# A new order for the instructions between the two projections of a token mixer, written by hand on four engines

## The chip, the core and the metric

One core of one Trainium2 chip runs the whole program. Its engines are TensorE (PE in the profile), VectorE (DVE), ScalarE (ACT), GpSimd (POOL) and SyncE (SP), and each has its own list of instructions that runs strictly in order. Engines wait for each other on semaphores. The metric is the device time of one execution in microseconds, taken as a median of several runs.

## What is computed

One inference step of a decoder with two layers, for 256 prompt tokens and 32 sample tokens (8 samples of 4), with shared weights. Each layer is a gated FFN, a token mixer and a second gated FFN. The mixer projects the tokens once, runs three groups of heads on the result and projects once more:

```python
gq, gk, gv, gg, glr, mu, mv, sq, sk, sv = split_cols(a @ w_in)
o_gla, s_gla = gla_mixer(gq, gk, gv, gg, glr, gla_w2, gla_b, gla_nw, gla_s0)
o_gm, v_gm = gmlp_mixer(mu, mv, gm_ln_w, gm_ln_b, gm_ws, gm_bs)
...
o_sb = sb_attend(hs(sq), kk, vv, pos0, sb_b).reshape(B, L, SB_W)
o = jnp.concatenate([o_gla, o_gm, o_sb], axis=-1) @ w_out
```

`gla_mixer` is gated linear attention in chunks of 64 tokens with a matrix state. `gmlp_mixer` is a causal spatial gate over chunks of 128. `sb_attend` is stick-breaking attention: with z the logits and a causal mask, the weights are `exp(log_sigmoid(z) + suffix)`, where `suffix` is the reverse running sum of `-softplus(z)`. Sample tokens attend to 1024 earlier keys and values of their own, which are gathered from a paged cache by a page table (8 heads, 64 wide, pages of 128 keys).

## The kernel before

All products run on TensorE; weights arrive as fp32, and ACT and DVE split each block into `w_hi` and `w_lo` (L1315, L1697), so that three products (L604 to L606) stand for one. Tokens lie along the free dimension, 288 of them (T). PSUM has eight banks, written `PS[:, bank, ...]`.

The change touches the stretch of each layer that lies between the last step of the mixer's input projection and the first product of its output projection (`first_out`, L666). Each of PE, ACT and DVE has an order written out by hand there, with helpers for each piece. No planner or queue chooses anything at run time. The helpers that the text names:

- Samples, in two groups of four samples, g = 0 and 1. DVE `sample_cap(g)`, ACT `sample_log1p_exp(g)` and DVE `sample_sums(g)` (the reverse scans, L1981) make the softplus and its running sums; PE `part_offsets(g)` and DVE `sample_offsets(g)` add the sums of later pages. ACT `sample_weights(g)` takes the exponential (L1475), DVE `turn_weights(g)` transposes in 32x32 blocks (L2001), PE `regroup(g)` moves blocks between partitions (L933), and ACT `weights_by_page(g)` copies the result to `a_keys` (L1482).
- PE `value_chunk(n)`, n = 0 to 15, eight of each group (L956): 4 pages of cached values times `a_keys`, summed in bank 4. Chunk n lies in slot n % 4 of the tile `direct`. SP's `page_chunk` (L486) issues four transfers of 256 KB for chunk n + 4 when chunk n has been used. `new_values(g)` (L967) adds the new tokens' values and ends the group; ACT `sample_rows(g)`, PE `turn_rows(g)` and ACT `sample_heads(g)` bring it into `Y`.
- Prompt, in four pairs of heads, p = 0 to 3. PE, DVE and ACT `prompt_scores(p)` (L1050, L2072, L1545), DVE `prompt_cap(p)`, ACT `prompt_log1p_exp(p)` (L1552, L1554), DVE `prompt_softplus(p)` (L2087), PE `prompt_sums(p)` (L1059, L1060), DVE `prompt_less(p)` (L2093), ACT `prompt_weights(p)` (L1559), PE `prompt_values(q)` (L1070, L1072).
- Linear attention: the gated q and k (L2100 to L2102), `gla_rows` (transposes of values and keys), the masked `att` (L1135, L2123), the state S (L1156, L2136 to L2141), the outputs in bank 6 and 7 (L1188 to L1207, 112 small products), their squares' sums (L1224, L1225), ACT's reciprocal root (L1366, L1368), and the samples' new state (L1242, L2188).
- Spatial gate: transposes of `dm` (L1099, L1105) and of the weights `wsr` (L1110), their mask (L2114), products (L1161, L1169, L1176), bias and gate (L2151, L2155, L2158).
- `rows_of(i, f0, bank, done)` (L1079) transposes 128 (or 32) tokens of keys or values; ACT `key_rows` and `value_rows` copy them out. GpSimd sends them to DRAM once the third copy of a kind is made, and the prompt's state once it is ready.

A wait names what must be done. Two kinds matter here: data, and PSUM banks that hold something still to be read (banks 0 to 3 serve the scores, `regroup`, `att`, the spatial gate and the prompt sums in turn).

## Time and profile before

| | us |
|---|---|
| median of 3 runs | 1393.45 |
| lowest and highest | 1392.14, 1394.14 |
| the profiled execution, its own time | 1392.76 |
| its span, first to last instruction | 1391.0 |
| stretch of the change, layer 0 | 384.36 to 447.69 |
| stretch of the change, layer 1 | 1058.27 to 1122.14 |
| mean granted clock of TensorE | 0.981 of full |

Times inside the trace count from the start of the span. "Idle before" is the time for which an engine had nothing to run before a group, and the name behind the arrow is what released it. A row "x64" of PE is 64 matmul records; an fp32 product is recorded as two. Ends of matmuls overlap the next start, so the distance from start to start is what a group costs.

### The profile page before, as it was taken

Reading aid. Unit: us, or ns where it says so; the run is one execution under the profiler, and the core shown is the slowest. Engines: PE = TensorE matmul, PEld = TensorE weight load, DVE = VectorE, ACT = ScalarE, POOL = GpSimd, SP = SyncE. Lnnn points to the kernel's source line nnn. Section 1 sums busy time; section 2 is a strip of 40 time slices with the busy share of each in tenths; the row PEclk is TensorE's granted clock in tenths of the full one; section 3 lists DMA queues with packets and bytes.
Section 4 is the critical chain, followed back from the end, with each engine's and each line's share of the span. In section 5 each row is a group of like instructions: output and inputs, shape, how many; then the busy total and the mean of one; then the engine's idle time right before and its main releaser. Section 6 shows DMA issues by size and latency. Waiting matters only on the chain.

```text
span 1391.0 us, 34449 instructions
## 1 busy us (share of the span) xinstructions
PE 1330.5 (96%) x13990; PEld 1269.4 (91%) x13990; DVE 810.3 (58%) x1188; ACT 587.9 (42%) x965; POOL 50.6 (4%) x131
## 2 busy tenths in 40 slices
PE   5999999999989899999999999999998998999997
PEld 4899999899966899999989999998997687999997
DVE  2554554668894655555465555447779557555544
ACT  2532243543565543333453333345336555333442
POOL 4000000000020000000000000001001000000000
PEclk9999999999999999999999999999999998999998
DMA  9978779789989895568876567987997993655552
GB/s 330 273 228 260 218 244 319 216 252 338 289 270 325 256 306 152 159 179 270 264 225 173 153 171 223 294 250 219 334 309 231 328 303 89 168 165 160 145 162 82
DMA packets 423816, 324.49 MB, mean 233 GB/s; under 512 B 15559, under 2 KB 351719, under 8 KB 423696
## 3 DMA queue, kind: packets, MB, share of 16 engines
q1 hardware_dynamic: 421124, 317.03, 75.1%
q0 software_dynamic: 2272, 5.61, 1.3%
q8 instruction: 90, 1.47, 0.4%
q14 instruction: 30, 0.25, 0.1%
q10 hardware_dynamic: 300, 0.13, 0.0%
HBM read 317.93 MB, written 4.78 MB: 232 GB/s over the span
## 4 chain that ended last, share of the span: by engine, by line
PE 85%; DVE 6%; ACT 3%; DMA 2%; SPq 2%; DVEq 2%; issue 1%; ACTq 0%
PE PS L604 23%; PE PS L605 23%; PE PS L606 23%; PE PS L632 3%; PE PS L910 2%; PE PS L666 2%; PE PS L667 1%; PE PS L668 1%; PE PS L956 1%; ACT Y L1373 1%; ACT xsq L1387 1%; DMA direct<-in_cache_sb_v 1%; SPq L486 1%; DMA raw<-in_ffn_w_in 1%; DMA xtok<-in_x_sample 1%
## 5 line engine op out<-in xcount | busy, mean ns | idle before, releaser
L1697 DVE TENSOR_TENSOR w_lo<-raw,w_hi 128x1024 fp32r<-128x1024 f32 (+1 forms) x368 | 392.9, 1106 | 443.6 <-ACT w_hi L1315 443.4
L1315 ACT ACTIVATE w_hi<-raw 128x1024 fp32r<-128x1024 f32 (+1 forms) x368 | 337.7, 960 | 659.3 <-PE PS L606 577.9
L604 PE MATMUL PS<-a_hi,w_hi 128*128 128x288 f32 x1760 | 524.0, 298 | 1.3 <-issue 1.3
L605 PE MATMUL PS<-a_lo,w_hi 128*128 128x288 f32 x1760 | 519.2, 295 | 0.0
L606 PE MATMUL PS<-a_hi,w_lo 128*128 128x288 f32 x1760 | 517.5, 294 | 0.0
L604 PEld LDWEIGHTS PS<-a_hi,w_hi 128*128 128x128 f32 x1760 | 329.8, 187 | 3.6 <-issue 3.3
L605 PEld LDWEIGHTS PS<-a_lo,w_hi 128*128 128x128 f32 x1760 | 330.4, 188 | 1.6 <-issue 1.4
L606 PEld LDWEIGHTS PS<-a_hi,w_lo 128*128 128x128 f32 x1760 | 331.4, 188 | 0.0
L605 PE MATMUL PS<-h_lo,w_hi 128*128 128x288 f32 x704 | 208.4, 296 | 0.0
L604 PE MATMUL PS<-h_hi,w_hi 128*128 128x288 f32 x704 | 208.1, 296 | 0.0
L606 PE MATMUL PS<-h_hi,w_lo 128*128 128x288 f32 x704 | 208.0, 296 | 0.0
L604 PEld LDWEIGHTS PS<-h_hi,w_hi 128*128 128x128 f32 x704 | 133.7, 190 | 0.4 <-issue 0.4
L606 PEld LDWEIGHTS PS<-h_hi,w_lo 128*128 128x128 f32 x704 | 132.0, 188 | 0.0
L605 PEld LDWEIGHTS PS<-h_lo,w_hi 128*128 128x128 f32 x704 | 131.9, 187 | 0.0
L1963 DVE STREAM_TRANSPOSE direct<-direct 128x2048 f32<-128x2048 f32 x32 | 72.2, 2289 | 0.0
L632 PE MATMUL PS<-direct,cT 128*32 128x128 f32 x1920 | 65.1, 289 | 7.0 <-issue 3.6
L632 PEld LDWEIGHTS PS<-direct,cT 128*32 128x32 f32 x1920 | 55.1, 117 | 12.3 <-issue 6.6
L666 PE MATMUL PS<-a_hi,w_hi 128*128 128x288 f32 x160 | 49.5, 309 | 5.5 <-DVE a_lo L1934 5.2
L667 PE MATMUL PS<-a_lo,w_hi 128*128 128x288 f32 x160 | 47.9, 299 | 0.0
L668 PE MATMUL PS<-a_hi,w_lo 128*128 128x288 f32 x160 | 47.8, 299 | 0.0
L1836 DVE TENSOR_TENSOR h_lo<-hf,h_hi 128x288 f32 (+1 forms) x88 | 40.3, 458 | 11.5 <-issue 9.5
L1831 DVE TENSOR_TENSOR hf<-sg,PS 128x288 f32<-128x288 f32 x88 | 39.4, 447 | 0.0
(323 smaller groups left out, 1131.0 us busy)
## 6 DMA issues: line engine op xcount, KB each, us to landing
raw<-in_ffn_w_in SPq DMA_DIRECT2D x176, 512.0 KB, 5.0
direct<-in_cond_w SPq DMA_DIRECT2D x240, 256.0 KB, 5.0
direct<-in_cache_sb_k SPq DMA_DIRECT2D x128, 256.0 KB, 4.3
direct<-in_cache_sb_v SPq DMA_DIRECT2D x128, 256.0 KB, 4.3
raw<-in_ffn_w_out SPq DMA_DIRECT2D x64, 384.0 KB, 3.8
raw<-in_mix_w_in SPq DMA_DIRECT2D x48, 512.0 KB, 7.0
raw<-in_ffn_w_out SPq DMA_DIRECT2D x64, 320.0 KB, 4.5
side<-in_cond_w SPq DMA_DIRECT2D x48, 256.0 KB, 5.3
```

The costliest lines, as they stand in the source:

```text
L604: pe.matmul(out, whi, hi, start=begins and i == 0, stop=False)
L605: pe.matmul(out, whi, lo, start=False, stop=False)
L606: last = pe.matmul(out, wlo, hi, start=False, stop=ends and i == n - 1)
L632: last = pe.matmul(PS[32 * g:32 * g + 32, 6 + pair, c * P:c * P + P], cT[:, 4 * half + kb, :], rows[:, kb * 512 + g * P:kb * 512 + g * P + P],
L666: pe.matmul(out, whi, a_hi[:, k, :], start=k == 0, stop=False)
L667: pe.matmul(out, whi, a_lo[:, k, :], start=False, stop=False)
L668: last = pe.matmul(out, wlo, a_hi[:, k, :], start=False, stop=k == KB - 1)
L1315: act.activation(w_hi[:, s, at_:at_ + n], raw[:, s, at_:at_ + n], ACT.Copy)\
L1697: tt(w_lo[:, s, at_:at_ + n], raw[:, s, at_:at_ + n], w_hi[:, s, at_:at_ + n], ALU.subtract).then_inc(lo_done.sem, 1)
L1831: tt(hf[:, s:s + 1, :], sg[:, s:s + 1, :], PS[:, 2 * s + 1:2 * s + 2, 0:T], ALU.mult)\
L1836: tt(h_lo[:, at_, :], hf[:, s:s + 1, :], h_hi[:, at_, :], ALU.subtract)\
L1963: dve.transpose(direct[:, n % 4, :], direct[:, n % 4, :]).then_inc(k_turned.sem, 1)
```

## The change

Only orders and waits change, and one PSUM location. No product, copy or transfer is added or dropped, and no shape changes; one drain of DVE between the spatial gate's bias and its gate goes, as other work now lies between them.

- PE: `regroup(0)` goes ahead of the second `rows_of` and its wait is for the second pair's scores, not for all four. `prompt_scores(2)` and `(3)` go behind it. `value_chunk(0)` goes ahead of `gla_rows` and of `att`; chunks 1 to 13 are spread anew. `part_offsets(1)` goes ahead of the samples' spatial gate. Chunks 5 to 7, `new_values(0)` and `regroup(1)` go ahead of the linear attention's outputs. `prompt_sums(0)`, `(1)` go behind them.
- The spatial gate's small sum for samples moves from bank 5 to bank 7, columns 256 on.
- ACT: `sample_weights(0)` ahead of the prompt scores, `weights_by_page(0)` ahead of the second `key_rows`, `sample_rows(0)` and `weights_by_page(1)` ahead of `value_rows(0)`; `values_by_sample` split into two calls with other work between them; `prompt_log1p_exp(2)` last before the root.
- DVE: `turn_weights(0)` ahead of the gated q and k, the spatial gate's copies and mask ahead of `prompt_scores(2)`, `sample_cap(1)` behind them, the masks of `att` ahead of `sample_sums(1)` (the scans), `sample_offsets(1)` and `turn_weights(1)` ahead of the state S, `prompt_softplus(0)` behind it, `prompt_less(0)` behind the outputs' squares.

```diff
@@ TensorE
-                prompt_scores(2)
-                prompt_scores(3)
                 pe.wait_ge(off_added.sem, off_added.at(l, 1))
...
                 rows_of(0, SK, 4, k_t)
+                pe.wait_ge(zp_off.sem, zp_off.at(l, 2))
+                regroup(0)
                 pe.wait_ge(kv_k.sem, kv_k.at(l, 1))
                 rows_of(1, SK, 4, k_t)
+                pe.wait_ge(a_copied.sem, a_copied.at(l, 1))
+                prompt_scores(2)
+                pe.wait_ge(kv_k.sem, kv_k.at(l, 2))
+                rows_of(2, SK, 4, k_t)
+                prompt_scores(3)
+                value_chunk(0)
+                pe.wait_ge(ws_got.sem, ws_got.at(l, 1))
+                turn_new(0)
                 pe.wait_ge(gla_in.sem, gla_in.at(l, 1))
                 pe.wait_ge(vn_got.sem, vn_got.at(l, 1))
                 gla_rows(0, 6)
-                pe.wait_ge(vn_got.sem, vn_got.at(l, 2))
-                gla_rows(1, 7)
                 pe.wait_ge(zp_off.sem, zp_off.at(l, PR))
-                regroup(0)
...
-                rows_of(2, SK, 4, k_t)
-                pe.wait_ge(gvk_a.sem, gvk_a.at(l, 1))
-                gla_rows(2, 6)
-                value_chunk(0)
-                value_chunk(1)
...
                 last.then_inc(att_sum.sem, 1)
+                pe.wait_ge(vn_got.sem, vn_got.at(l, 2))
+                gla_rows(1, 7)
+                value_chunk(1)
+                pe.wait_ge(gvk_a.sem, gvk_a.at(l, 1))
+                gla_rows(2, 6)
+                value_chunk(2)
                 pe.wait_ge(new_spread.sem, new_spread.at(l, 1))
                 rows_of(2, SV, 5, v_t)
-                value_chunk(2)
+                value_chunk(3)
...
-                value_chunk(3)
+                value_chunk(4)
...
                 last.then_inc(gs_sum.sem, 1)
+                value_chunk(5)
+                part_offsets(1, 5)
                 pe.wait_ge(wss_ready.sem, wss_ready.at(l, 1))
...
                 last.then_inc(gs_sum.sem, 1)
-                part_offsets(1, 5)
-                prompt_sums(0, 0)
-                value_chunk(4)
+                value_chunk(6)
+                value_chunk(7)
+                new_values(0)
+                pe.wait_ge(gm_y.sem, gm_y.at(l, 2))
+                regroup(1)
+                pe.wait_ge(off_added.sem, off_added.at(l, 2))
+                rows_of(0, SV, 5, v_t)
...
                 last.then_inc(o_sum.sem, 1)
-                value_chunk(5)
-                pe.wait_ge(gm_y.sem, gm_y.at(l, 2))
-                prompt_sums(1, 2)
-                pe.wait_ge(off_added.sem, off_added.at(l, 2))
-                rows_of(0, SV, 5, v_t)
-                value_chunk(6)
-                value_chunk(7)
-                pe.wait_ge(c_sub.sem, c_sub.at(l, 2))
-                regroup(1)
-                new_values(0)
+                value_chunk(8)
+                prompt_sums(0, 0)
                 pe.wait_ge(kv_v.sem, kv_v.at(l, 2))
                 rows_of(1, SV, 5, v_t)
+                value_chunk(9)
+                prompt_sums(1, 2)
+                value_chunk(10)
...
                 turn_new(1)
+                value_chunk(11)
                 pe.wait_ge(new_spread.sem, new_spread.at(l, 2))
                 turn_rows(0)
-                value_chunk(8)
+                pe.wait_ge(c_sub.sem, c_sub.at(l, 1))
                 prompt_sums(2, 0)
-                value_chunk(9)
-                value_chunk(10)
-                value_chunk(11)
+                value_chunk(12)
+                pe.wait_ge(c_sub.sem, c_sub.at(l, 2))
                 prompt_sums(3, 2)
...
-                value_chunk(12)
                 value_chunk(13)
@@ ScalarE
+                sample_weights(0)
                 prompt_scores(0)
                 prompt_scores(1)
-                sample_weights(0)
                 key_rows(0, 4)
+                weights_by_page(0)
                 key_rows(1, 4)
+                key_rows(2, 4)
...
                 gla_rows(0, 6)
-                weights_by_page(0)
-                key_rows(2, 4)
+                gla_rows(2, 6)
                 prompt_log1p_exp(0)
-                gla_rows(2, 6)
                 value_rows(2, 1)
                 prompt_log1p_exp(1)
-                values_by_sample()
+                values_by_sample(0)
                 sample_weights(1)
+                sample_rows(0)
+                weights_by_page(1)
                 value_rows(0, 2)
+                values_by_sample(1)
+                value_rows(1, 3)
                 prompt_log1p_exp(2)
-                weights_by_page(1)
-                sample_rows(0)
-                value_rows(1, 3)
@@ VectorE
                 prompt_scores(0)
                 prompt_scores(1)
-                sample_cap(1)
+                turn_weights(0)
                 dve.wait_ge(gate_e.sem, gate_e.at(l, 1))
...
-                turn_weights(0)
-                prompt_scores(2)
-                prompt_scores(3)
...
                    causal[:, :].unsqueeze(1).to_broadcast([P, GH, P]), ALU.mult).then_inc(ws_got.sem, 1)
+                prompt_scores(2)
+                prompt_scores(3)
+                sample_cap(1)
+                prompt_cap(0)
+                prompt_cap(1)
...
                 spread_new(0)
-                sample_sums(1)
-                prompt_softplus(0)
                 dve.wait_ge(att_sum.sem, att_sum.at(l, 1))
...
                 last.then_inc(att_ready.sem, 1)
+                sample_sums(1)
+                dve.wait_ge(wss_sum.sem, wss_sum.at(l, 1))
...
+                sample_offsets(1, 5)
...
+                turn_weights(1)
                 dve.wait_ge(s_sum.sem, s_sum.at(l, 1))
...
                 last.then_inc(s_ready.sem, 1)
...
+                prompt_softplus(0)
                 tt(Y[:, 2:4, :], Y[:, 2:4, :], Fm[:, MU:MU + 2, :], ALU.mult).then_inc(gm_done.sem, 1)
-                sample_offsets(1, 5)
                 prompt_softplus(1)
-                prompt_less(0)
-                prompt_cap(2)
-                turn_weights(1)
...
                 tt(gt[2][:, :, :], gt[0][:, :, :], gt[0][:, :, :], ALU.mult).then_inc(o_sq.sem, 1)
+                prompt_less(0)
+                prompt_cap(2)
                 prompt_less(1)
                 prompt_cap(3)
```

Ahead of `sample_offsets(1)` DVE now has the mask of the samples' spatial weights, and behind it the two bias additions, which it had behind the state S before.

## Rows read from the trace of the kernel before

**Rows 1.** Page, engines: busy time, share of the span, instructions.
```profile
PE 1330.5 (96%) x13990; PEld 1269.4 (91%) x13990; DVE 810.3 (58%) x1188; ACT 587.9 (42%) x965; POOL 50.6 (4%) x131
```
**Rows 2.** Windows over both stretches: length, busy per engine, PEclk, DMA share, GB/s.
```profile
384.30:447.60 63.30, 56.06 (x960) 41.10 (x958) 44.33 (x78) 37.30 (x81) 9.27 (x15) 0.92 0.89 296
1058.20:1122.10 63.90, 56.54 (x960) 41.57 (x958) 44.01 (x78) 37.37 (x82) 9.30 (x15) 0.92 0.89 296
```
**Rows 3.** Timeline of PE, layer 0: start, us, group, idle before and releaser.
```profile
394.68 0.66 PE L1086 MATMUL PS<-ident,Fm 128*128 128x128 f32 x2 [2.56 <-DVE vn L2108]
...
399.67 2.17 PE L956 MATMUL PS<-direct,a_keys 128*32 128x128 f32 x64
...
411.10 1.08 PE L956 MATMUL PS<-direct,a_keys 128*32 128x128 f32 x32
412.11 1.09 PE L1188 MATMUL PS<-att,gvk 128*64 128x128 f32 x16
...
416.29 1.09 PE L956 MATMUL PS<-direct,a_keys 128*32 128x128 f32 x32
...
433.69 0.91 PE L1059 MATMUL PS<-sn,suffix 128*128 128x384 f32 x2
...
435.62 1.93 PE L1242 MATMUL PS<-vm,gvk 32*64 32x512 f32 x8
...
440.31 1.08 PE L956 MATMUL PS<-direct,a_keys 128*32 128x128 f32 x32 [1.62 <-DMA direct<-in_cache_sb_v]
...
447.69 0.40 PE L666 MATMUL PS<-a_hi,w_hi 128*128 128x288 f32 x1
```
**Rows 4.** Timeline of PE, layer 1.
```profile
1113.60 1.94 PE L956 MATMUL PS<-direct,a_keys 128*32 128x128 f32 x32 [1.53 <-DMA direct<-in_cache_sb_v]
...
1118.62 0.44 PE L1072 MATMUL PS<-zp,sv 128*64 128x128 f32 x4
...
1122.14 0.37 PE L666 MATMUL PS<-a_hi,w_hi 128*128 128x288 f32 x1 [0.21 <-DVE a_lo L2203]
```
**Rows 5.** Timeline of ACT, layer 0.
```profile
388.49 1.06 ACT L1475 ACTIVATE z<-z 128x1024 f32<-128x1024 f32 x1
...
397.89 1.21 ACT L1482 ACTIVATE a_keys<-PS 128x256 f32<-128x256 f32 x4 [0.71 <-PE PS L933]
...
426.56 0.69 ACT L1366 ACTIVATE gt<-PS,eps 128x512 f32<-128x512 f32 x1 [0.28 <-PE PS L1225]
...
431.56 0.84 ACT L1554 ACTIVATE sn<-sn 128x768 f32<-128x768 f32 x1
```
**Rows 6.** Timeline of DVE, layer 0.
```profile
391.16 1.23 DVE L2001 STREAM_TRANSPOSE a_turn<-z 128x1024 f32<-128x1024 f32 x1
...
432.44 0.96 DVE L2087 SCALAR_TENSOR_TENSOR sn<-zp,sn 128x768 f32<-128x768 f32 x1 [0.84 <-ACT sn L1554]
...
438.20 0.95 DVE L2093 SCALAR_TENSOR_TENSOR zp<-zp,PS 128x768 f32<-128x768 f32 x1
```
**Rows 7.** SP's line L486 over chunk 4's issues, then over chunk 10's, with landing times.
```profile
L486 SPq DMA_DIRECT2D direct<-in_cache_sb_v x4: 333/356/358, 401.2 to 402.8; - x4
...
DMA to landing us min/median/max: 3.8/4.2/4.8
...
L486 SPq DMA_DIRECT2D direct<-in_cache_sb_v x4: 332/333/333, 422.6 to 424.1; - x4
...
DMA to landing us min/median/max: 2.7/3.4/4.6
```
**Rows 8.** Windows before and in two stretches of lower clock, columns as in the second group.
```profile
413.80:417.20 3.40, 3.40 (x114) 3.17 (x108) 1.85 (x4) 0.00 (x0) 0.00 (x0) 1.00 1.04 379
417.20:420.60 3.40, 3.40 (x15) 2.08 (x8) 0.27 (x1) 0.00 (x0) 0.00 (x0) 0.50 0.64 152
...
1110.10:1113.50 3.40, 1.63 (x36) 0.81 (x32) 1.98 (x3) 1.22 (x2) 0.00 (x0) 1.00 1.03 381
1113.50:1116.90 3.40, 3.30 (x42) 2.45 (x44) 0.00 (x0) 1.52 (x2) 0.00 (x0) 0.51 1.05 357
```

More of the change, by code:

```diff
@@ L1160, in _ @@
                 pe.sem_inc(gvk_seen.sem, 1)
-                pe.matmul(PS[0:NS, 5, 0:GH * TS], rep[:, :, :].rearrange("s b t -> s (b t)"),
+                pe.matmul(PS[0:NS, 7, 256:256 + GH * TS], rep[:, :, :].rearrange("s b t -> s (b t)"),
                           wst[0:TS, :, 0:TS], start=True, stop=True).then_inc(wss_sum.sem, 1)
-                value_chunk(3)
+                value_chunk(4)
                 pe.wait_ge(att_ready.sem, att_ready.at(l, 2))
@@ L1574, in key_rows, with values_by_sample @@
                     act.activation(kst[0:n, i, :], PS[0:n, bank, :], ACT.Copy).then_inc(kv_k.sem, 1)
-                def values_by_sample():
-                    for j in range(GP):
-                        for b in range(B):
-                            last = act.activation(vm[j][:, b, :], gvk[0:NS, 2, j * P:j * P + P], ACT.Copy,
-                                                  scale=same_s[:, b:b + 1])
-                        last.then_inc(vm_ready.sem, 1)
+                def values_by_sample(j):
+                    for b in range(B):
+                        last = act.activation(vm[j][:, b, :], gvk[0:NS, 2, j * P:j * P + P], ACT.Copy,
+                                              scale=same_s[:, b:b + 1])
+                    last.then_inc(vm_ready.sem, 1)
                 def sample_rows(g):
@@ L2110, in _ @@
                 cp(vn[0:NS, 2, :], PS[0:NS, 7, 0:GW]).then_inc(vn_got.sem, 1)
-                prompt_cap(0)
-                prompt_cap(1)
                 dve.wait_ge(ws_t.sem, ws_t.at(l, 1))
@@ L2131, in _ @@
                 last.then_inc(att_ready.sem, 1)
+                sample_sums(1)
+                dve.wait_ge(wss_sum.sem, wss_sum.at(l, 1))
+                tt(wss[:, :, :].rearrange("s h (b t) -> s h b t", t=TS),
+                   PS[0:NS, 7, 256:256 + GH * TS].rearrange("s (h t) -> s h t", h=GH).unsqueeze(2)
+                   .to_broadcast([NS, GH, B, TS]),
+                   same_s[:, :].unsqueeze(1).unsqueeze(3).to_broadcast([NS, GH, B, TS]), ALU.mult)\
+                    .then_inc(wss_ready.sem, 1)
+                sample_offsets(1, 5)
+                dve.wait_ge(bs_in.sem, bs_in.at(l, 1) * 64)
+                dve.wait_ge(gs_sum.sem, gs_sum.at(l, 1))
+                tt(Y[:, 2:4, 0:NP].rearrange("p j (i t) -> p j i t", i=PT_),
+                   PS[:, 2, :].rearrange("p (i j t) -> p j i t", i=PT_, j=GP),
+                   bs[:, :, :].unsqueeze(2).to_broadcast([P, GP, PT_, P]), ALU.add).then_inc(gm_y.sem, 1)
+                dve.wait_ge(gs_sum.sem, gs_sum.at(l, 2))
+                tt(sample(Y, 2, 4), PS[:, 3, 0:GP * NS].rearrange("p (j b t) -> p j b t", j=GP, t=TS),
+                   bs[:, :, 0:TS].unsqueeze(2).to_broadcast([P, GP, B, TS]), ALU.add).then_inc(gm_y.sem, 1)
+                turn_weights(1)
                 dve.wait_ge(s_sum.sem, s_sum.at(l, 1))
@@ L2142, in _ @@
                 last.then_inc(s_ready.sem, 1)
-                dve.wait_ge(wss_sum.sem, wss_sum.at(l, 1))
-                tt(wss[:, :, :].rearrange("s h (b t) -> s h b t", t=TS),
-                   PS[0:NS, 5, 0:GH * TS].rearrange("s (h t) -> s h t", h=GH).unsqueeze(2)
-                   .to_broadcast([NS, GH, B, TS]),
-                   same_s[:, :].unsqueeze(1).unsqueeze(3).to_broadcast([NS, GH, B, TS]), ALU.mult)\
-                    .then_inc(wss_ready.sem, 1)
-                dve.wait_ge(bs_in.sem, bs_in.at(l, 1) * 64)
-                dve.wait_ge(gs_sum.sem, gs_sum.at(l, 1))
-                tt(Y[:, 2:4, 0:NP].rearrange("p j (i t) -> p j i t", i=PT_),
-                   PS[:, 2, :].rearrange("p (i j t) -> p j i t", i=PT_, j=GP),
-                   bs[:, :, :].unsqueeze(2).to_broadcast([P, GP, PT_, P]), ALU.add).then_inc(gm_y.sem, 1)
-                dve.wait_ge(gs_sum.sem, gs_sum.at(l, 2))
-                tt(sample(Y, 2, 4), PS[:, 3, 0:GP * NS].rearrange("p (j b t) -> p j b t", j=GP, t=TS),
-                   bs[:, :, 0:TS].unsqueeze(2).to_broadcast([P, GP, B, TS]), ALU.add).then_inc(gm_y.sem, 1)
-                dve.drain()
+                prompt_softplus(0)
                 tt(Y[:, 2:4, :], Y[:, 2:4, :], Fm[:, MU:MU + 2, :], ALU.mult).then_inc(gm_done.sem, 1)
-                sample_offsets(1, 5)
                 prompt_softplus(1)
-                prompt_less(0)
-                prompt_cap(2)
-                turn_weights(1)
                 dve.wait_ge(o_sum.sem, o_sum.at(l, 1))
```

3 lines of the change are left out of this document (removed).

## The prediction

> **What bounds the kernel now.** I read the page's engine rows first: TensorE is busy for 96% of the span [rows 1], so time is won only where TensorE waits or runs slowly. Then the windows over the two stretches that the change touches. They last 63.3 and 63.9 us, 9% of the span together. TensorE is busy for 56.1 and 56.5 us of them, and its granted clock there is 0.92 [rows 2]: the mean of 2.4 GHz and of some 10 us at 1.2 GHz. So in each stretch 7.3 us are idle, and up to 5 us of the busy time are lost to the low clock. The timeline of PE says where. In layer 0 it stands 2.56 us for a copy of DVE before `gla_rows(0)`, and 1.62 us near the end for a value chunk's transfer [rows 3]; layer 1 has 1.53 us of the latter [rows 4]. The other waits are under 0.9 us each.
>
> The transfers are a second chain. SP may ask for chunk n + 4 only when chunk n is used. The first chunk starts at 399.67 and takes 1.0 us, half of the pair's row [rows 3]; SP's next request goes out at 401.2 [rows 7]. Behind the stretch, the output projection and the FFN are products back to back, so a microsecond won at the first product of the output projection, 447.69 in layer 0 and 1122.14 in layer 1 [rows 3, 4], is won in full. I subtract 673.91, the distance between the stretches' starts, from layer 1's times: its 1122.14 is then 448.23.
>
> **The change, followed through.** Nothing is computed less. I lay the new orders out with start-to-start distances of this trace: an instruction starts when its engine is free and its last wait is over, some 0.05 us after the releaser's end. All times are layer 0's, at the full clock.
>
> *Up to the first chunk.* PE's part offsets, first two scores and 14 transposes are packed from 384.4 to 388.3. ACT now does `sample_weights(0)` right behind the gates' exponentials, at 387.15 (388.49 before, 1.06 us and a small one [rows 5]), to 388.3. DVE turns them at 388.4 instead of 391.16 (1.23 us [rows 6]), to 389.6. PE regroups for 0.5 us, ACT copies for 1.2 us [rows 5], to 391.5. Then PE has two scores of 0.75 us, a transpose group of 0.45 between them and a wait of 0.15: `value_chunk(0)` at 393.7, 6.0 us before today's 399.67. SP's next request falls at 395.1 instead of 401.2.
>
> *Up to the outputs of the linear attention.* PE waits 0.65 us for ACT's `gla_rows(0)`, which lies behind two activations of 1.05 us for samples. Chunks 1 to 4 start at 397.4, 399.5, 400.9 and 402.7. Then the transfers are late. An unloaded chunk needs 1.5 us from first to last issue and up to 4.6 from there to landing, 6.1 in all [rows 7]. Chunk 4 shares the engines with GpSimd's copy of the keys, which goes out about 0.9 us ahead of it now as then: 1.6 + 4.8 = 6.4 us [rows 7]. Loaded, the engines move 379 GB/s [rows 8], so chunks of 1.05 MB land 2.7 to 2.8 us apart. Chunk 4 lands at 401.6, chunk 5 at 405.0 (3.4 us later, the keys' copy taking its share), 6 at 407.8, 7 at 410.5. PE waits some 0.3, 0.8 and 1.7 us for 5, 6 and 7, which it uses early now. Chunk 7 (1.0), `new_values(0)`, `regroup(1)` and a transpose (2.2 us) follow, so the outputs start at 413.7. DVE is no bound there: the state is ready at 412.1.
>
> *The Trainium skill on this point.* "DMA: Bandwidth & Descriptors" gives about 2.0 us of fixed cost for one transfer (section "Anatomy of one DMA") and about 358 GB/s from DRAM for one core (section "Specifications"). An estimate by it is 2.0 + 1.05 MB / 358 GB/s = 4.9 us for an unloaded chunk. The trace has 6.1 us [rows 7], and under load a higher rate [rows 8]. By the page's figure chunk 7 would land some 0.8 us earlier, and the sum below would be 1.6 us better over two layers. I go by the rows.
>
> *From the outputs to the end.* The 112 small products take 416.29 - 412.11 = 4.2 us [rows 3]: to 417.9. Then chunk 8, prompt sum 0, a transpose group, chunk 9, sum 1, chunk 10 (3 x 0.97 + 2 x 1.9 + 0.45 = 7.2 us; a sum is 435.62 - 433.69 [rows 3]) and the squares' sums, 1.0 us, end at 426.1. Today they end at 426.3, just before ACT's root [rows 5], so up to here the transfer waits have eaten the 6 us. From here a chain through ACT and DVE rules: root, two weights, sample heads and `prompt_log1p_exp(3)`, from 426.56 to 432.40 today [rows 5], then softplus, 0.96 us [rows 6]. It reaches the last prompt sum at 426.1 + 0.2 + 5.9 + 1.0 = 433.2, with PE idle for 2.1 us ahead of it (today 433.69). That sum and the states' product (1.9 + 1.93 us [rows 3]) end at 437.0. `prompt_less(3)` ends 439.15 - 437.55 = 1.6 us behind the latter [rows 3, 6], at 438.6; ACT's weights last to 439.5; the second `prompt_values` starts at 439.7 (0.1 us for the semaphores) and takes 1.35, to 441.0. From its end to `first_out`, a path of rounding through ACT and DVE, lie 1122.14 - 1119.0 = 3.15 us [rows 4]; PE's last chunks (2.9 us) fit in. Result: 444.2. The gain is 3.5 us in layer 0 and 4.0 us in layer 1, 7.5 together. Nearly all of it is the transfer waits at today's end, with the slow stretch behind layer 1's: chunks 12 to 15 are now asked for over 5 us before they are needed.
>
> *The clock.* This sum has no slow stretch. Today the clock fell to half in both layers behind the small products of the outputs, in layer 0 from 417.2 to 420.6 [rows 8], though TensorE was busy without a break before. At half speed 3.4 us delay full work by 1.7 us. The new order leaves the 112 products in one block, so I take one such stretch per layer, -3.4 us. What remains is 7.5 - 3.4 = 4.1 us. Bounds: none (7.5), and one more in each layer (below).
>
> *Moved at no cost.* GpSimd's copies of keys, values and state follow their tiles; the keys' copy is counted above, the others lie in the transfers' spare time. If they did not, each takes 0.6 MB / 379 GB/s = 1.5 us. The output weights' split on ACT waits for those copies, which end earlier. `values_by_sample` in two parts costs nothing: ACT stands idle for over 4 us before `value_rows(1)`. `wss` in bank 7 meets nothing that is still read.
>
> **The rivals.**
> A: as laid out, one slow stretch per layer; 4.1 us faster.
> B: fewer slow stretches, or chunks 6 and 7 in time. For it: `regroup` and two scores now break up the run of transposes ahead of today's first slow stretch; and without the transfer waits the outputs would start with the state at 412.1 instead of 413.7, 1.6 us per layer. Against it: rows 7 and 8. 5.7 to 7.5 us faster.
> C: the transfer wait brings a slow stretch. The waits for chunks 6 and 7 leave PE two thirds idle for 3.4 us, and in layer 1 the clock was 0.51 right behind such a stretch with its wait of 1.53 us [rows 4, 8]. One fall more in each layer costs 0.8 to 1.6 us (the table's shift, by where it begins), 2.4 together: 1.7 us faster, within what can be told from no change.
> D, the other side: the clock. If it falls more often than today, in the early block of transposes and scores too (1.4 to 2.4 us per layer, as the first chunk then comes that much later or the end of the block runs at half speed) and behind the transfer waits, that is 2.4 + 3 to 5 us more than A: 1.3 to 3.3 us slower. It decides from three falls per layer on. Against it: that block is 6 us shorter than today's.
>
> **How the numbers follow.** The profiled execution took 1392.76 us, 1.76 more than its span; the median is 0.69 above it. A gives 1392.76 - 4.1 = 1388.7 for such an execution, and 1393.45 - 4.1 = 1389.4 against the median. Chances: A 0.38, B 0.20, C 0.27, D 0.15. A measurement of this kernel can tell about 0.2%, 2.8 us, from no change. A (but for 0.05, a little less gained) and B are faster by that: 0.53. C, that 0.05 and the milder third of D are within it, 0.36 with rounding; slower is 0.11. The range reaches from B's 1393.45 - 7.5 = 1386.0 to D's milder end, 1393.45 + 1.3 = 1394.8.
>
> **What the profile would show.** Chunk 0 near 393.7 and SP's next request near 395; waits for transfers before chunks 6 and 7, and none before 12 to 15; the outputs (L1188) near 413.7; a clock of 0.5 behind them; the squares' sums ending at 426 to 428; PE idle for about 2 us before the last prompt sum; `first_out` at 444 to 446. The forecast is wrong if chunk 0 is late, if chunk 7 lands far from 410.5, or if the clock falls in more or fewer places.

## The result, and the profile after

The changed kernel takes 1405.32 us (median of 4 runs, 1402.98 to 1406.27) against 1393.12 us (4 runs, 1392.14 to 1394.14): a ratio of 1.0094, 95% interval 1.0082 to 1.0107. It is 0.9% slower; the forecast was 1389.4, at most 1394.8. Here and below a ratio and its interval are over the fast executions of both kernels, so it can differ by up to 0.15% from the quotient of the two medians beside it. The profiled execution took 1404.54 us, 11.8 more than that of before. The page's row of the engines, which answers to [rows 1], has 10 us more of busy TensorE for the same 13990 matmuls:

```profile
PE 1340.7 (96%) x13990; PEld 1274.7 (91%) x13990; DVE 810.0 (58%) x1188; ACT 587.6 (42%) x965; POOL 50.8 (4%) x131
```

Windows of the changed kernel: both stretches of the change (these answer to [rows 2]), then three places in them in order of time, each the piece ahead of a slow stretch and the slow stretch itself, and last the end of layer 1's. The columns are those of [rows 2].

```profile
386.47:454.70 68.23, 60.50 (x960) 42.62 (x958) 43.60 (x76) 37.06 (x81) 9.41 (x15) 0.87 0.84 277
1065.28:1133.80 68.52, 59.41 (x960) 42.06 (x958) 43.53 (x76) 36.99 (x81) 9.43 (x15) 0.90 0.84 279
...
409.50:412.90 3.40, 1.34 (x40) 0.96 (x38) 2.90 (x4) 1.16 (x2) 0.00 (x0) 0.99 0.98 346
412.90:416.30 3.40, 2.98 (x58) 1.87 (x62) 3.18 (x10) 0.00 (x0) 0.74 (x2) 0.50 1.05 402
419.70:423.10 3.40, 3.40 (x111) 3.11 (x106) 1.48 (x3) 1.75 (x6) 0.00 (x0) 1.00 0.99 369
423.10:426.50 3.40, 3.40 (x12) 2.16 (x9) 0.20 (x1) 0.00 (x0) 0.00 (x0) 0.50 0.65 196
...
436.80:440.20 3.40, 1.25 (x23) 0.74 (x12) 1.40 (x2) 2.14 (x3) 0.00 (x0) 0.99 1.04 396
440.20:450.40 10.20, 10.20 (x63) 5.40 (x62) 2.24 (x3) 2.73 (x3) 0.00 (x0) 0.50 0.38 130
1116.00:1119.40 3.40, 1.25 (x20) 0.75 (x12) 1.36 (x2) 2.10 (x3) 0.00 (x0) 1.00 1.06 393
1119.40:1129.60 10.20, 10.20 (x65) 5.40 (x65) 2.24 (x3) 2.74 (x3) 0.00 (x0) 0.50 0.38 129
```

Counted up to `first_out`, 0.3 to 0.4 us behind the end of these windows, the stretches have grown from 63.3 and 63.9 us to 68.6 and 68.9. TensorE's granted clock in them is 0.87 and 0.90, where both had 0.92. Summed over the granted-clock records, TensorE ran at 1.2 GHz for 17.1 us of the one and 13.7 us of the other, against 10.2 us in each before. The slow stretches are five over both layers in either kernel; they have become longer. The longest is new: 10.2 us at the end of each layer's stretch, during which TensorE had work without a break, behind a piece of 3.4 us in which it had work for only 1.25.

The timeline of PE in the changed kernel, layer 0 (answers to [rows 3]; L1197 is what was L1188, L1246 what was L1242):

```profile
396.03 1.08 PE L956 MATMUL PS<-direct,a_keys 128*32 128x128 f32 x32
...
407.55 1.08 PE L956 MATMUL PS<-direct,a_keys 128*32 128x128 f32 x32 [0.88 <-DMA direct<-in_cache_sb_v]
...
410.17 1.08 PE L956 MATMUL PS<-direct,a_keys 128*32 128x128 f32 x32 [0.41 <-DMA direct<-in_cache_sb_v]
413.32 1.94 PE L956 MATMUL PS<-direct,a_keys 128*32 128x128 f32 x32 [2.07 <-DMA direct<-in_cache_sb_v]
...
417.94 1.09 PE L1197 MATMUL PS<-att,gvk 128*64 128x128 f32 x16
...
431.10 1.13 PE L1228 MATMUL PS<-gt,head_ones 128*128 128x512 f32 x2
...
439.41 0.88 PE L1059 MATMUL PS<-sn,suffix 128*128 128x384 f32 x2 [2.15 <-DVE sn L2090]
...
442.36 3.68 PE L1246 MATMUL PS<-vm,gvk 32*64 32x512 f32 x8
...
455.04 0.37 PE L666 MATMUL PS<-a_hi,w_hi 128*128 128x288 f32 x1 [0.21 <-DVE a_lo L2205]
```

and the same in layer 1, which answers to [rows 4]:

```profile
1088.57 1.08 PE L956 MATMUL PS<-direct,a_keys 128*32 128x128 f32 x32 [1.69 <-DMA direct<-in_cache_sb_v]
...
1093.82 1.08 PE L956 MATMUL PS<-direct,a_keys 128*32 128x128 f32 x32 [1.53 <-DMA direct<-in_cache_sb_v]
...
1118.57 0.88 PE L1059 MATMUL PS<-sn,suffix 128*128 128x384 f32 x2 [2.15 <-DVE sn L2090]
...
1121.43 3.68 PE L1246 MATMUL PS<-vm,gvk 32*64 32x512 f32 x8
...
1134.20 0.37 PE L666 MATMUL PS<-a_hi,w_hi 128*128 128x288 f32 x1 [0.21 <-DVE a_lo L2205]
```

All orders came out as written down: chunk 0 lies 9.6 us after the stretch's start (15.3 before), the transfer waits at the end are gone, and those before chunks 5 to 7 are there. What is new is the price of the wait before the last prompt sum. It is 2.15 us long, as forecast. But 0.8 us behind its end the clock falls, and the states' product behind it takes 3.68 us instead of 1.93.

Counted from each stretch's own start (386.47 and 1065.28), set against the forecast's (its times less 384.36):

| us from the stretch's start | forecast | layer 0 | layer 1 |
|---|---|---|---|
| chunk 0 | 9.3 | 9.6 | 9.6 |
| linear attention's outputs begin | 29.3 | 31.5 | 31.8 |
| squares' sums begin | 40.7 (full clock) | 44.6 | 45.0 |
| last prompt sum begins | 48.8 | 52.9 | 53.3 |
| `first_out` | 59.8 | 68.6 | 68.9 |

Of the 11.8 us, 10.3 lie in the two stretches (5.2 and 5.1). The other 1.5 us are a later start of layer 0's stretch, by 2.1 us, less 0.3 us between the stretches and 0.3 behind them. The change doesn't touch that early part, and in other executions of kernels with the same code there the stretch began between 384.7 and 387.4.

### The profile page after: what moved, and what is told of

Same layout as the page of the kernel before. It is cut to its first block, busy times and chain, and to the rows that moved or that the text cites. A ratio compares the mean times of both kernels' runs of the same rounds, so it can differ in the third digit from the quotient of the medians.

```text
span 1402.8 us, 34451 instructions
## 1 busy us (share of the span) xinstructions
PE 1340.7 (96%) x13990; PEld 1274.7 (91%) x13990; DVE 810.0 (58%) x1188; ACT 587.6 (42%) x965; POOL 50.8 (4%) x131
## 4 chain that ended last, share of the span: by engine, by line
PE 84%; DVE 4%; ACT 4%; DMA 3%; SPq 3%; issue 1%; DVEq 1%; ACTq 0%
PE PS L604 23%; PE PS L605 22%; PE PS L606 22%; PE PS L632 3%; PE PS L666 2%; SPq L486 2%; PE PS L910 1%; PE PS L667 1%; PE PS L668 1%; PE PS L956 1%; ACT Y L1376 1%; ACT xsq L1390 1%; PE PS L1059 1%; DVE w_lo L1700 1%; DMA direct<-in_cache_sb_v 1%
## 5 line engine op out<-in xcount | busy, mean ns | idle before, releaser
L632 PE MATMUL PS<-direct,cT 128*32 128x128 f32 x1920 | 68.4, 298 | 5.9 <-issue 3.7
L956 PE MATMUL PS<-direct,a_keys 128*32 128x128 f32 x1024 | 36.7, 289 | 7.4 <-DMA direct<-in_cache_sb_v 7.4
```

Source lines behind the costliest of these rows:

```text
L632: last = pe.matmul(PS[32 * g:32 * g + 32, 6 + pair, c * P:c * P + P], cT[:, 4 * half + kb, :], rows[:, kb * 512 + g * P:kb * 512 + g * P + P],
L956: last = pe.matmul(PS[32 * p:32 * p + 32, 4, smp * P:smp * P + P], a_keys[:, 4 * half + t, 32 * p:32 * p + 32], direct[:, n % 4, 512 * t + ...
```

## The experiments

Three theories were set against each other. The *clock*: new waits and light work bring TensorE to 1.2 GHz more often and for longer. The *chain*: what ACT and DVE still have to do sets the end, and the clock only shows it. The *transfers*: value chunks that arrive late delay all that follows. Every ratio is against the kernel before on the same chip.

"Filler" below is a 128x128 by 128x256 fp32 product of constants into a PSUM bank that is free at that time; nothing reads it. It is pure extra work for TensorE.

**Chunks in the wait.** The changed kernel, with two value chunks ahead of the last prompt sum.

```diff
                 value_chunk(12)
+                value_chunk(13)
+                value_chunk(14)
                 pe.wait_ge(c_sub.sem, c_sub.at(l, 2))
                 prompt_sums(3, 2)
...
-                value_chunk(13)
...
-                value_chunk(14)
```

> The changed kernel with value chunks 13 and 14 moved ahead of the last prompt sum, into the 2.15 us for which TensorE waits there. Theory 1 (the wait lets the clock fall, and the states' product behind it is too light to bring it back, so 10.2 us run at half speed in each layer): the clock stays at 1.0 up to the output projection and about 4 to 5 us per layer come back, 1395 to 1398 us against 1405.3. Theory 2 (the chain through ACT and DVE sets the end whatever the clock): within 1 us of 1405.3. Theory 3 (late transfers, chunks 4 to 7): no change either, 1404 to 1406.

Measured: 1400.72 us against 1390.85, ratio 1.0066 (1.0047 to 1.0085), less gain than the 1395 to 1398 that the clock theory expected; the time alone hardly sets it apart from the changed kernel (1.0079 when that ran again, below). The profile does. The wait for DVE shrinks to at most 0.2 us (in layer 0 chunk 14 now waits 0.88 us for its transfer there), and there is no slow stretch behind it: from the last prompt sum to `first_out` it is 11.1 us in both layers, where the changed kernel took 15.6. But `first_out` now waits 1.8 us for DVE's `a_lo`, since the moved chunks no longer fill the time in front of it, and slow stretches remain: 3.4 us behind the outputs in each layer, 3.4 us at the transfer waits in layer 0.

**Filler in the wait.** The same place, with nothing moved.

```diff
                 value_chunk(12)
                 pe.wait_ge(c_sub.sem, c_sub.at(l, 2))
+                for _ in range(4):
+                    pe.matmul(PS[:, 2, 0:NP], ones[:, :], vecs[:, :, :].rearrange("p a b -> p (a b)"), start=True, stop=True)
                 prompt_sums(3, 2)
```

> The changed kernel with four products of ones by a constant tile (256 columns, fp32, about 1.7 us, result unused) in front of the last prompt sum, and no other move. It is pure extra work. Theory 1: the clock stays up and 4 to 5 us per layer come back all the same, 1395 to 1398 us. Theories 2 and 3: the same as the changed kernel or slower by up to 1 us, 1405 to 1407.

Measured: 1396.7 us against 1390.85, ratio 1.0044 (1.0024 to 1.0064). Windows of this kernel over both stretches, and the longer of the two slow pieces that are left in layer 0:

```profile
386.98:454.20 67.22, 60.57 (x969) 43.68 (x967) 44.04 (x77) 37.27 (x82) 9.42 (x15) 0.90 0.85 284
1064.00:1126.50 62.50, 56.44 (x969) 41.35 (x967) 44.06 (x77) 37.26 (x82) 9.43 (x15) 0.97 0.92 305
413.40:423.60 10.20, 9.39 (x120) 6.05 (x120) 4.25 (x12) 4.57 (x14) 1.21 (x2) 0.50 1.03 381
```

Behind the last prompt sum the clock stays up and the 11.1 us are back in both layers; layer 1's stretch is 6.4 us shorter than the changed kernel's. In layer 0 the slow piece behind the waits for chunks 6 and 7 is 10.2 us long in this execution, 3.4 in the changed kernel's, and each layer still has 3.4 us behind the outputs (from 427.1 and 1099.5). The wait before the last sum is one place of three.

**The same wait in the kernel before.** Two chunks taken from in front of its last prompt sum.

```diff
                 value_chunk(9)
-                value_chunk(10)
-                value_chunk(11)
                 prompt_sums(3, 2)
...
+                value_chunk(10)
+                value_chunk(11)
                 value_chunk(12)
```

> The kernel of before with value chunks 10 and 11 moved from ahead of the last prompt sum to behind the states' product, so that TensorE waits about 2 us there too. Theory 1: a stretch of 0.5 clock appears behind the wait and costs 2 to 5 us per layer, 1397 to 1403 us against 1393.1. Theory 2: at most 1 us slower, since the chunks then fill the later wait for transfers. Theory 3: up to 2 us slower per layer, if the later use of chunks 10 and 11 delays the requests for 14 and 15; then the waits for transfers grow and the clock ahead of them stays at 1.0.

Measured: 1404.11 us against 1390.85, ratio 1.008 (1.0055 to 1.0105). The timeline of PE in this kernel, layer 0 and then layer 1:

```profile
437.64 1.29 PE L1059 MATMUL PS<-sn,suffix 128*128 128x384 f32 x2 [1.83 <-DVE sn L2087]
438.72 0.63 PE L1060 MATMUL PS<-sn,ones 128*128 128x128 f32 x2
...
454.63 1.54 PE L956 MATMUL PS<-direct,a_keys 128*32 128x128 f32 x32 [2.72 <-DMA direct<-in_cache_sb_v]
...
1119.82 0.91 PE L1059 MATMUL PS<-sn,suffix 128*128 128x384 f32 x2 [1.83 <-DVE sn L2087]
1120.57 0.38 PE L1060 MATMUL PS<-sn,ones 128*128 128x128 f32 x2
```

The wait is there in both layers (1.83 us). In layer 0 the sum's `ones` product right behind it takes 0.63 us in place of 0.38: 1.2 GHz, for 3.4 us. In layer 1 the same wait brought no fall; the next slow piece there begins 14.6 us behind it, at a transfer wait. The test isn't clean either, because the later chunks make the transfer waits grow to 4.0 and 4.4 us per layer. It shows that such a wait can bring a fall in the old order too; it doesn't price it.

**GpSimd's copy of the keys later.** Only in the queue of GpSimd; in the changed kernel, and further below in the one with all fillers.

```diff
-                after(kv_k, l, 3)
-                rows_out(kst, k_prompt, k_sample, k_out)
                 after(s_ready, l, 1)
...
+                after(kv_k, l, 3)
+                rows_out(kst, k_prompt, k_sample, k_out)
```

> The changed kernel with GpSimd's copy of the keys to DRAM (0.6 MB) sent behind the prompt's state instead of ahead of value chunk 4's transfer. Theory 3: chunks 4 to 7 land 1.5 us earlier, TensorE's waits for them (3.4 us in layer 0, 4.1 in layer 1) shrink by as much, and the outputs start 1.5 to 2 us earlier: 1401 to 1403 us. Theory 1 alone: the fall at the last prompt sum stays, and what is won ahead of it comes through or not by the phase of the clock: 1402 to 1406.

Measured: 1410.82 us against 1390.85, ratio 1.0147 (1.0097 to 1.0197), from three executions of 1408.15 to 1414.44 us; a fourth took 3273 us for a reason that I don't know and is left out. No theory had expected more than 1406. The transfer waits are 2.3 and 4.1 us where they were 3.4 and 4.0, so they are 1.1 us shorter in one layer and no shorter in the other. In this profile TensorE was at 1.2 GHz for 20.5 and 27.3 us of the stretches. In layer 1 one fall lies in the early block, from 1071.7, and chunk 0 comes 1.5 us later for it; so this run can't tell what the copy costs.

**Filler in all new waits.** As in the second experiment, and 2, 1 and 4 such products ahead of chunks 5, 6 and 7.

```diff
+                for _ in range(2):
+                    pe.matmul(PS[:, 0, 0:NP], ones[:, :], vecs[:, :, :].rearrange("p a b -> p (a b)"), start=True, stop=True)
                 value_chunk(5)
...
+                for _ in range(1):
+                    pe.matmul(PS[:, 0, 0:NP], ones[:, :], vecs[:, :, :].rearrange("p a b -> p (a b)"), start=True, stop=True)
                 value_chunk(6)
+                for _ in range(4):
+                    pe.matmul(PS[:, 0, 0:NP], ones[:, :], vecs[:, :, :].rearrange("p a b -> p (a b)"), start=True, stop=True)
                 value_chunk(7)
```

> The kernel with the filler in the gap, with seven more filler products (0.4 us each, result unused) in TensorE's waits ahead of value chunks 5, 6 and 7. Theory 1 (every wait of some 2 us lets the clock fall, and the fall costs more than the wait): no stretch of 0.5 between the first chunk and the outputs, though they start no earlier than the transfers allow, 30.0 us after the stretch's start; the spread over runs shrinks; 1393 to 1396 us. Theory 3 (the transfers themselves cost the time): no change against the kernel with the one filler, 1396.7.

Measured: 1390.47 us (10 runs) against 1391.85, ratio 0.999 (0.9976 to 1.0004). Its windows over the stretches, and over the pieces that were slow in the changed kernel or stood ahead of them:

```profile
386.80:448.20 61.40, 58.20 (x983) 42.69 (x981) 44.07 (x77) 37.28 (x82) 9.44 (x15) 1.00 0.95 310
1058.60:1120.20 61.60, 58.26 (x981) 42.48 (x981) 43.99 (x77) 37.23 (x82) 9.46 (x15) 1.00 0.92 308
409.50:412.90 3.40, 3.40 (x51) 2.69 (x51) 2.47 (x4) 1.16 (x2) 0.00 (x0) 1.00 0.98 337
412.90:416.30 3.40, 3.12 (x74) 1.89 (x75) 3.18 (x10) 0.07 (x1) 0.25 (x1) 1.00 1.05 398
420.00:423.40 3.40, 3.40 (x92) 2.92 (x89) 1.00 (x3) 0.84 (x3) 0.00 (x0) 1.00 1.03 383
440.20:450.40 10.20, 9.65 (x157) 7.29 (x154) 8.35 (x11) 5.63 (x8) 1.83 (x2) 1.00 0.67 211
```

and its timeline of PE around the last prompt sum:

```profile
414.09 1.08 PE L956 MATMUL PS<-direct,a_keys 128*32 128x128 f32 x32 [0.28 <-DMA direct<-in_cache_sb_v]
...
434.94 1.99 PE L1247 MATMUL PS<-vecs,ones 128*128 128x256 f32 x8
437.07 0.91 PE L1059 MATMUL PS<-sn,suffix 128*128 128x384 f32 x2
...
439.00 1.93 PE L1254 MATMUL PS<-vm,gvk 32*64 32x512 f32 x8
...
448.17 0.37 PE L666 MATMUL PS<-a_hi,w_hi 128*128 128x288 f32 x1 [0.55 <-DVE a_lo L2213]
```

Eleven products more per layer make the changed kernel about 1% faster. In this execution no slow piece is left in either stretch of the change, the one behind the outputs included, whose 112 small products weren't touched. They last 61.3 and 61.7 us. The slow piece behind the outputs doesn't always stay away, as the run with the keys' copy late shows further below. This result decides for the clock and against the chain: ACT and DVE have no work less, and TensorE has some 5.5 us more per layer (11 products of 0.5 us). The second experiment and this one share the cost out: from 1.0094 (1.0079 when the changed kernel ran again, below) to 1.0044 for the wait before the last sum, 5 to 7 us, and from 1.0044 to 0.999 for those before chunks 5 to 7, 7.5 us. By the intervals each of these is uncertain by about 3 us.

**The outputs broken up.** The first experiment's kernel, with chunk 8 and prompt sum 0 between the small products; then also chunk 1 right behind chunk 0, to have the transfers sooner.

```diff
                 last.then_inc(o_sum.sem, 1)
+                value_chunk(8)
                 pe.wait_ge(s0_in.sem, s0_in.at(l, 1) * 32)
...
+                prompt_sums(0, 0)
                 for b in range(B):
...
-                value_chunk(8)
-                prompt_sums(0, 0)
```

and for the second of them:

```diff
                 value_chunk(0)
+                value_chunk(1)
...
                 gla_rows(1, 7)
-                value_chunk(1)
```

> The kernel with chunks 13 and 14 in the gap, and with value chunk 8 and prompt sum 0 moved in between the 112 small products of the linear attention's outputs, where they are ready. Theory 1: no fall of the clock behind the outputs, 1.7 us less per layer, 1396 to 1398 us against 1400.7. Theory 2 (dependences set the time): within 1 us of 1400.7.

> The previous kernel with value chunk 1 right behind chunk 0, as in the kernel of before. It frees slot 1 about 2.7 us earlier. Theory 3: chunk 5's request goes out right behind chunk 4's, chunks 5 to 7 land 1 us earlier and the outputs start 1 us earlier: 1394 to 1396 us. Without it: DVE's mask of att comes 1 us later and eats the gain, 1396 to 1398 us.

Measured: 1399.25 us, ratio 1.0055 (1.0037 to 1.0073), and 1396.33 us, ratio 1.0031 (1.0016 to 1.0047), both against 1391.85. The first can't be told from the 1.0066 without the new split. The slow pieces weren't gone: in the first of them they lie from 408.5 to 415.3 and from 1087.7 to 1097.9, around the waits for chunks 5 to 7. Layer 0 has 3.4 us more, from 425.5, right behind the outputs although these are broken up; the same is so in the second, from 425.8. With chunk 1 early the transfer waits are still 3.8 us in layer 0 and 2.2 in layer 1, where a fall in the early block (from 1070.9) had delayed chunk 0 by 1.4 us; the outputs begin 31.9 and 33.1 us after the start. Chunk 7 was used 27.4 and 28.2 us after the start, without the early chunk 27.7 and 27.0: asking for one chunk sooner isn't seen to bring chunk 7 sooner.

**The kernel before, its outputs broken up.** Chunk 5 and prompt sum 1 between the small products.

```diff
                 last.then_inc(o_sum.sem, 1)
+                value_chunk(5)
                 pe.wait_ge(s0_in.sem, s0_in.at(l, 1) * 32)
...
+                pe.wait_ge(gm_y.sem, gm_y.at(l, 2))
+                prompt_sums(1, 2)
                 for b in range(B):
...
-                value_chunk(5)
-                pe.wait_ge(gm_y.sem, gm_y.at(l, 2))
-                prompt_sums(1, 2)
```

> The kernel of before with value chunk 5 and prompt sum 1 moved in between the small products of the outputs. Theory 1: the fall of the clock behind the outputs in both layers goes, 1.7 us each, and the next chunks are asked for earlier, so 2 to 4 us faster than before, 1387 to 1389 us. If the fall comes from something else: within 1 us of before.

Measured: 1391.24 us (11 runs) against 1391.85, ratio 0.9993 (0.9982 to 1.0004). Windows of both stretches:

```profile
385.70:447.30 61.60, 54.04 (x961) 40.10 (x959) 43.86 (x77) 37.53 (x82) 9.29 (x15) 0.97 0.90 306
1058.10:1120.00 61.90, 53.49 (x961) 39.83 (x959) 43.88 (x77) 37.35 (x82) 9.32 (x15) 0.97 0.93 305
```

In its profile 3.4 us at 1.2 GHz are left per layer, at the transfer wait near the end. The slow stretch behind the outputs is gone, but so is the one in the early block (393.3 to 400.2 and 1069.2 to 1072.6 in the kernel before), which the edit doesn't touch. So what breaking up the outputs does isn't shown by this one profile. The stretches are 1.8 and 2.0 us shorter than in [rows 2]; the medians don't tell this from no change.

**The changed kernel once more**, unaltered, for its spread.

> The changed kernel unaltered, on the chip of the next three. All theories: 1.007 to 1.012 of before. Theory 1 expects falls of the clock in its waits again, but not all at the same places as in the first profile.

Measured: 1400.92 us (1397.62 to 1408.94) against 1391.68, ratio 1.0079 (1.0049 to 1.0109). This execution holds the cleanest comparison of all. Its two windows over the places behind the last prompt sum, layer 0's and layer 1's (with the piece ahead of it), and the timeline of PE, layer 0's wait first:

```profile
438.90:449.10 10.20, 10.20 (x64) 5.41 (x64) 2.24 (x3) 2.74 (x3) 0.00 (x0) 0.50 0.41 144
1114.50:1118.40 3.90, 1.78 (x36) 1.19 (x35) 2.61 (x4) 3.43 (x8) 0.00 (x0) 1.00 1.06 399
1118.40:1128.60 10.20, 10.17 (x152) 6.77 (x152) 5.80 (x7) 4.41 (x6) 0.00 (x0) 1.00 0.68 222
```

```profile
437.97 0.88 PE L1059 MATMUL PS<-sn,suffix 128*128 128x384 f32 x2 [2.15 <-DVE sn L2090]
...
1118.43 0.88 PE L1059 MATMUL PS<-sn,suffix 128*128 128x384 f32 x2 [2.15 <-DVE sn L2090]
...
1120.33 1.93 PE L1246 MATMUL PS<-vm,gvk 32*64 32x512 f32 x8
...
1129.50 0.37 PE L666 MATMUL PS<-a_hi,w_hi 128*128 128x288 f32 x1 [0.55 <-DVE a_lo L2205]
```

The wait is the same 2.15 us in both layers. In layer 0 the clock fell behind it; in layer 1 it didn't, and from the last prompt sum to `first_out` it took 1129.50 - 1118.43 = 11.1 us, as forecast; in layer 0 it took 15.5. The fall costs 4.5 us, with the same instructions and the same wait. Over all profiles that have this wait (the changed kernel twice, and with the keys' copy late) it came in five of six stretches.

**The keys' copy late, with all fillers.** The kernel with all fillers and the edit of the fourth experiment.

> The kernel with all fillers, and GpSimd's copy of the keys sent behind the state's. The clock is held up, so this shows what the transfers alone cost. Theory 3: chunks 5 to 7 land 1 to 1.5 us earlier, but the fillers and the state on DVE allow the outputs only some of it, 0.5 to 1 us per layer: 1388.5 to 1390 us. If the keys' copy doesn't hold the chunks up: within 0.5 us of 1390.5.

Measured: 1392.01 us against 1391.68, ratio 1.0003 (0.9989 to 1.0016); 1390.47 and 0.999 without the edit. Chunk 7 was used 28.0 and 27.1 us after the start, against 27.3 and 27.4 without the edit, so the copy of the keys isn't seen to delay it. But the clock wasn't full, as the expectation had it. Both layers had a slow piece right behind the outputs:

```profile
421.80:425.20 3.40, 3.40 (x8) 2.19 (x9) 0.05 (x1) 0.00 (x0) 0.00 (x0) 0.51 1.03 369
1094.20:1097.60 3.40, 3.40 (x18) 1.94 (x7) 0.00 (x0) 0.00 (x0) 0.00 (x0) 0.50 0.96 338
```

TensorE's instructions are those of the kernel with all fillers, whose profile had none there. The fillers make falls rarer; they don't rule them out.

**No falls, with the outputs broken up.** The changed kernel with chunks in the wait and between the small products, and the seven filler products ahead of chunks 5 to 7.

> The changed order with chunks 13 and 14 in the gap, the outputs broken up by chunk 8 and prompt sum 0, and fillers only ahead of chunks 5 to 7. Theory 1: no fall of the clock in the stretch, 61 us from its start to the output projection, 1388 to 1391 us. Theory 2: no better than the kernel with all fillers, as 1.8 us of rounding wait stay at the end.

Measured: 1395.31 us against 1391.68, ratio 1.0029 (1.0014 to 1.0043). The profiled execution is the fastest of the ten (1392.11 us, span 1390.4) and has no slow piece in the stretches. They last 62.8 and 62.6 us, 1.8 of them a wait for `a_lo` at the end. That is about 1 us per layer more than with filler in the wait, from which I would have expected 1393. The other executions show where the rest goes: the profiled one has the highest granted clock of the ten, 0.990, and the three slowest, 1398.97 to 1400.11 us, have 0.984 and 0.985, that is some 15 us more at 1.2 GHz. Where those falls lie, no trace shows.

**The kernel before, outputs broken up, and filler at its transfer wait.**

```diff
                 value_chunk(12)
-                value_chunk(13)
                 pe.wait_ge(c_sub.sem, c_sub.at(l, 3))
+                for _ in range(4):
+                    pe.matmul(PS[:, 0, 0:NP], ones[:, :], vecs[:, :, :].rearrange("p a b -> p (a b)"), start=True, stop=True)
+                value_chunk(13)
                 prompt_values(0, 0)
```

The edit also puts the wait for the third pair's `prompt_less` ahead of chunk 13.

> The order of before with the outputs broken up by chunk 5 and prompt sum 1, and four filler products in the wait for chunk 13's transfer. Theory 1: no fall at the end either, 0.5 to 1.5 us less per layer than with the outputs alone broken up: 1388 to 1390 us against 1391.2. Theory 3: the transfers set this end, no change.

Measured: 1392.66 us against 1391.68, ratio 1.0007 (0.9997 to 1.0018). The slow piece at the transfer wait is gone, but others stand further ahead (3.4 us at 396.3, 6.8 at 1068.8, 3.4 at 1096.1), so the two stretches are 62.6 and 62.8 us. Filler at one wait doesn't keep the clock up at another.

Not all of the clock theory's sizes came. It had the kernel with filler in the wait right (1395 to 1398), and the repeat. With all fillers the kernel was faster than expected; with chunks in the wait, with the wait put into the old order, with the outputs broken up (except where chunk 1 was early) and in the last three the kernels were slower, by 1 to 4 us.

## Why the prediction was wrong, step by step

*Up to the first chunk:* right. 9.6 us after the start against 9.3, nearly 6 us sooner than before.

*The transfers up to chunk 7:* right in kind, too small in size. Waits of 0.3, 0.8 and 1.7 us were expected. Layer 0 had 0.88, 0.41 and 2.07, layer 1 0.4 (before chunk 4), 1.69, 0.43 and 1.53: 3.4 and 4.0 us in place of 2.8. Chunk 7 was used 26.9 and 28.5 us after the start instead of 26.1. The fixed cost of 2.0 us that the prediction took from the Trainium skill's page "DMA: Bandwidth & Descriptors", section "Anatomy of one DMA", belongs there to transfers that GpSimd issues; SP issues the chunks. The sum didn't use it. With layer 0's chunk 7 at half speed (1.94 us for 1.08), the outputs began 2.1 and 2.5 us late.

*From the outputs to the last prompt sum:* right. Outputs to squares' sums took 13.2 us: the forecast's 11.4 and 1.8 for its one slow stretch (1.7 forecast), which came where it was put in both layers. From there to the last prompt sum it was 8.3 us against 8.1, with the wait of 2.15 against 2.1.

*From the last prompt sum on:* here the forecast failed, in its paragraph "The clock". It took one slow stretch of 3.4 us per layer, behind the outputs, where it had itself read some 10 us at 1.2 GHz per layer in the old order; why the rest should go, that paragraph doesn't say (only rival B has a reason, for the early block). Measured were 17.1 and 13.7 us. And it left the wait that it had found before the last prompt sum at its bare 2.1 us. I had forecast that TensorE would be two thirds idle around the waits of chunks 6 and 7 and made a rival of it (C), at a price of 0.8 to 1.6 us whose working the forecast doesn't show; in layer 0, which had this fall, chunk 7 took 0.86 us longer. The wait before the last sum leaves it as idle: 1.25 of 3.4 us busy. What follows is 10.2 us at 1.2 GHz, and 11.0 us of forecast became 15.6, in both layers. Those 4.6 us, 1.8 of the slow stretch behind the outputs, 0.2 of the chain and 2.1 to 2.5 of late outputs are the whole distance from 59.8 to 68.6 and 68.9.

The Trainium skill's page "TensorE: Matmul & The Clock Gate", section "HAM oscillation — how this bites in real kernels", describes this kind of loss: short bursts of products with waits for transfers between them, each burst then run at the low clock. The trace agrees in kind, at shorter waits than the page's example has, and also behind a wait that is for DVE and not for a transfer: 2.15 us before the last prompt sum, and 10.2 us at clock 0.50 behind it.

*Rival D*, at 0.15, had the sign and the cause, the clock, but neither the size nor the way: 10.3 us slower in the stretches where D had 1.3 to 3.3, and by longer slow stretches, not by more of them. D had looked for the further falls in the early block of transposes, where this execution had none, and behind the transfer waits, where layer 0 had one; the dearest came behind a wait for DVE.

*The gain at full clock*, 7.5 us, was too high also by itself. With no slow piece left, the new order needs 61.3 and 61.7 us, 2.0 and 2.2 less than before and not 3.5 and 4.0; the fillers may cost some of that, and no run shows how much. The old order with its outputs broken up needs 61.6 and 61.8, with 3.4 us at the low clock in each. So even with the clock on its side the new order is only 0.2 us per layer shorter than the old one. Chunk 0 comes 6 us sooner, but the transfers bound what follows: in the kernel with all fillers chunk 7 starts 27.3 us after the start, 1.2 behind the forecast's, and the outputs at 30.5, where the kernel before has them at 27.8.

*Over all executions* and not only those with a profile: the mean granted clock was 0.972 to 0.981 in the 8 of the changed kernel, and 0.983 to 0.991 in the 10 with all fillers. The kernel before, in 74 executions on three chips, had 0.979 to 0.988. So the new order with fillers spends less time at 1.2 GHz than the old one and is still no faster.

Open is what decides whether the clock falls behind a given wait: in one execution 2.15 us brought a fall in layer 0 and none in layer 1, and 1.83 us did the same in the old order. Open too is what makes the clock differ between executions of one kernel; in the last but one, whose median is 3.2 us above its profiled execution, the time follows it. No version here is faster than the kernel before by more than can be told.

## What to carry to other kernels

A wait of TensorE costs its own length and then, often, what the clock takes: here 2.15 us of waiting was followed by 10.2 us at 1.2 GHz in five stretches of six, and where a stretch with the fall and one without stand in one execution it cost 4.5 us more. When an order is laid out by hand, list TensorE's waits, here those from about 1.5 us on, and price each as a possible fall. To see whether a loss is the clock or the chain, put unused products into the waits: if extra work makes the kernel faster, it was the clock. One profile isn't enough to say that a slow stretch is cured; look at the granted clock of several executions. Work pulled ahead of its transfers only moved the wait forward here.

## What the hardware did that I had not expected

- TensorE stayed at 1.2 GHz for 10.2 us in which it was busy without a break (the windows of the changed kernel from 440.20 and 1119.40). That work was the prompt sum's end, the states' product (8 records with 32 rows, 3.68 us) and value chunks. The same instructions begun at full clock stayed there (layer 1 of the changed kernel's second profile).
- The 112 small products were followed by a slow stretch in both layers of the changed kernel, with TensorE busy for all of the 3.4 us before. In the kernel with all fillers the same block (417.34 to 421.52, TensorE just as busy) was followed by none, see the window from 420.00; with the same products of TensorE and the keys' copy late it was followed by one in both layers again (windows from 421.80 and 1094.20). The block alone doesn't decide it.
- With filler at one place, a fall at another could be longer than without it: 10.2 us from 413.4 in the second experiment, where the changed kernel had 3.4 from 412.9. In the old order the falls of the early block (393.3, 1069.2) were absent in the profile with the outputs broken up and back in the last (396.3, 1068.8), with the same instructions there.
- The transfers' rate reached 402 GB/s over 3.4 us (412.9 to 416.3), above the 379 on which the forecast's spacing of the chunks rested.
